# Input norm of a two-layer streaming encoder computed with tokens as rows; last-head results kept on the chip past a block; early features loaded in two places

## What is computed

```python
def rms_norm(x, g):
    xf = x.astype(jnp.float32)
    y = xf * lax.rsqrt(jnp.mean(xf * xf, axis=-1, keepdims=True) + EPS)
    return (y * g.astype(jnp.float32)).astype(x.dtype)

hp = rms_norm(yp, norm_g[l])                      # first step of layer 0
u, a_raw, b_raw, z_a, q_b, k_b, v_b, z_b = _split(h @ w_in, L0_SPLITS)
...
S_new, o_a = blocked_scan(gdn_block, S0, (q_a, k_a, v_a, g, beta), CHUNK)
...
y = jnp.concatenate([o_a, o_b], axis=-1) @ w_out  # layer 0
...
return o @ w_out, S_new                           # layer 1
```

## Time and profile before

| | |
|---|---|
| median of 3 runs | 3609.12 us (3608.56 to 3609.76) |
| profiled execution, its own time | 3610.31 us |
| its span, first to last instruction | 3608.6 us, 47321 instructions |
| mean granted TensorE clock | 0.99 of full |
| busy: TensorE, its weight loads | 3499.8, 2577.4 us |
| busy: VectorE, ScalarE, GpSimd | 1178.3, 1095.7, 533.1 us |

### The profile page before, as it was taken

How to read it: one execution, slowest core, us unless ns; L and a number is a source line. 1 busy time by engine, 2 the same in 40 slices (tenths; PEclk the granted TensorE clock), 3 DMA queues, 4 the chain that set the end, 5 groups by cost and what they waited for, 6 DMA issues and landing times. The chain is left out here.

```text
span 3608.6 us, 47321 instructions
## 1 busy us (share of the span) xinstructions
PE 3499.8 (97%) x16631; PEld 2577.4 (71%) x16631; DVE 1178.3 (33%) x2993; ACT 1095.7 (30%) x2794; POOL 533.1 (15%) x527
## 2 busy tenths in 40 slices
PE   8999999999799999999999998999999999899999
PEld 5777777777477878777766675677777777566676
DVE  3555545555223333333320234022222122220223
ACT  2443333333134334344210242122223222210242
POOL 3443345444000000000001002000000000011000
PEclk9999999999999999999999999999999999999999
DMA  5211411112412231122261102111111111371101
GB/s 145 60 38 32 31 28 34 32 37 84 102 39 43 44 42 30 43 46 90 89 198 47 36 13 79 41 30 44 39 50 44 37 36 33 117 230 47 35 1 48
DMA packets 246025, 206.85 MB, mean 57 GB/s; under 512 B 19903, under 2 KB 222943, under 8 KB 245831
## 3 DMA queue, kind: packets, MB, share of 16 engines
q1 hardware_dynamic: 239902, 194.16, 21.2%
q10 hardware_dynamic: 5936, 10.34, 0.8%
HBM read 158.49 MB, written 45.99 MB: 57 GB/s over the span
## 5 line engine op out<-in xcount | busy, mean ns | idle before, releaser
L497 PE MATMUL gdn_pj<-hT,Wb 128*128 128x352 f32 x1536 | 516.3, 462 | 3.0 <-PEq L45 3.0
L1999 PE MATMUL gla_pj<-hT,Wb 128*128 128x352 f32 x1536 | 471.9, 461 | 6.5 <-PEq L45 5.9
L1449 PE MATMUL band_pj<-hT,Wb 128*128 128x384 f32 (+1 forms) x1152 | 387.1, 465 | 16.8 <-PEq L45 13.8
L1999 PEld LDWEIGHTS gla_pj<-hT,Wb 128*128 128x128 f32 x1536 | 290.9, 191 | 156.8 <-issue 8.7
L497 PEld LDWEIGHTS gdn_pj<-hT,Wb 128*128 128x128 f32 x1536 | 266.3, 192 | 92.1 <-issue 5.5
L1449 PEld LDWEIGHTS band_pj<-hT,Wb 128*128 128x128 f32 x1152 | 207.2, 192 | 99.7 <-issue 19.5
L1995 PE MATMUL gla_pj<-gla_Wv,hT 128*128 128x256 f32 (+1 forms) x1152 | 266.8, 381 | 0.0
L1995 PEld LDWEIGHTS gla_pj<-gla_Wv,hT 128*128 128x128 f32 x1152 | 217.2, 190 | 31.8
L1634 ACT ACTIVATE band_E<-band_NS,band_nm 128x576 f32<-128x576 f32 (+9 forms) x136 | 89.8, 660 | 216.0 <-DVE band_nm L1712 215.9
L1211 POOL TENSOR_TENSOR x_kept<-gdn_AT,gdn_level 128x384 f32<-128x384 f32 x144 | 144.2, 1032 | 35.8 <-DVE gdn_TT L993 18.5
L1479 PE MATMUL band_pj<-Wb,hT 128*128 128x128 f32 x1152 | 144.2, 275 | 0.0
(11 more groups left out here) (410 smaller groups left out, 5490.3 us busy)
## 6 DMA issues: line engine op xcount, KB each, us to landing
Wb<-in_l_w_in_dram SPq DMA_DIRECT2D x96, 512.0 KB, 6.2
fin_xT<-x_features SPq DMA_DIRECT2D x16, 528.0 KB, 7.6
fin_R<-o_features SPq DMA_DIRECT2D x16, 528.0 KB, 9.7
Wb<-in_l_w_mkv_dram SPq DMA_DIRECT2D x8, 1024.0 KB, 5.5
Wb<-in_l_w_out_dram SPq DMA_DIRECT2D x16, 512.0 KB, 4.4
gla_Wv<-in_l_w_in_dram SPq DMA_DIRECT2D x8, 1024.0 KB, 5.4
o_features<-gla_OF ACTq DMA_DIRECT2D x14, 528.0 KB, 6.0
gdn_GB<-gate_rows SPq DMA_DIRECT2D x8, 544.0 KB, 3.7
```

What stands on the lines that cost most here:

```text
L497: mm = pe.matmul(pj[:, m % 2, 0:w], W[:, j, k, :], hT[:, k, c0:c0 + w], start=k == 0, stop=k == KD - 1)
L1449: mm = pe.matmul(out[:, 0:w], W[:, BAND_SLOT[j], k, :], hT[:, k, c0:c0 + w], start=k == 0, stop=k == KD - 1)
L1999: mm = pe.matmul(pj[:, m % 2, 0:w], W[:, SLOT[kind], k, :], hT[:, k, c0:c0 + w], start=k == 0, stop=k == KD - 1)
```

## The change

*Entry.* The norm is taken with tokens as rows, before the transposition. ScalarE squares the tile as it was loaded, with the row sum as second output, and takes logarithm and exponential of one column; VectorE scales the tile by it into `xN`; TensorE transposes both `xS` (for `x_kept`) and `xN` (for `hT`); VectorE multiplies the latter by the gain on its way out of PSUM. ScalarE copies seven of the nine tiles to `x_kept`, VectorE tiles 2 and 5. GpSimd and the matrix of ones are no longer used. 

```diff
+                def normed(t):
+                    pe.wait_ge(scaled, t + 1)
+                    wait(pe, h_out, t - 1)
                     for k in range(KD):
-                        mm = pe.matmul(PS[:, t % 2, 0:rows(t)], ones[:, :], sq[:, t % 2, k, 0:rows(t)], start=k == 0, stop=k == KD - 1)
-                    mm.then_inc(summed, 1)
+                        mm = pe.transpose(TH[:, t % 2, k, 0:r], xN[0:r, t % 2, 128 * k:128 * k + 128], ident[0:r, 0:r])
+                    mm.then_inc(h_turned, 1)
...
+                    act.wait_ge(x_ld[t], 16)
+                    wait(act, squared, t)
+                    act.activation(sq[0:r, :], xS[0:r, t, :], ACT.Square, accum_out=ss[0:r, t:t + 1]).then_inc(squared, 1)
+                    act.wait_ge(squared, t + 1)
+                    act.activation(rs[0:r, t:t + 1], ss[0:r, t:t + 1], ACT.Ln, scale=1.0 / D, bias=eps[0:r, 0:1]).then_inc(rooted, 1)
+                    act.wait_ge(rooted, t + 1)
+                    act.activation(rs[0:r, t:t + 1], rs[0:r, t:t + 1], ACT.Exp, scale=-0.5).then_inc(rs_ok, 1)
...
-                    pool.tensor_tensor(sq[:, t % 2, :, 0:rows(t)], xT[:, :, cols(t)], xT[:, :, cols(t)], ALU.mult).then_inc(squared, 1)
...
+                def out(t):
+                    dve.wait_ge(h_turned, t + 1)
+                    dve.tensor_tensor(hT[:, :, cols(t)], TH[:, t % 2, :, 0:r], g[:, :].unsqueeze(2).broadcast_to([128, KD, r]),
+                                      ALU.mult).then_inc(h_out, 1)
...
-                    for k in range(KD):
-                        mm = dve.scalar_tensor_tensor(hT[:, k, cols(t)], xT[:, k, cols(t)], g[:, k:k + 1], rs[:, t % 2, 0:r],
-                                                      ALU.mult, ALU.mult)
-                    mm.then_inc(h_out, 1)
+                    wait(dve, h_turned, t - 1)
+                    dve.tensor_scalar(xN[0:r, t % 2, :], xS[0:r, t, :], rs[0:r, t:t + 1], None, ALU.mult).then_inc(scaled, 1)
+                    if t:
+                        out(t - 1)
+                    if t in BY_DVE:
+                        dve.wait_ge(x_turned, t + 1)
+                        dve.tensor_copy(xT[:, :, cols(t)], TX[:, t % 2, :, 0:r]).then_inc(x_dve, 1)
```

```diff
-                sp.wait_ge(st_p, H_A * 16)
-                sp.wait_ge(st_s, H_A * 16)
-                sp.wait_ge(st_o, H_A * 32)
+                sp.wait_ge(st_p, (H_A - 1) * 16)
+                sp.wait_ge(st_s, (H_A - 1) * 16)
+                sp.wait_ge(st_o, (H_A - 1) * 32)
...
-                act.dma_start(state_p[last:H_A, :, :].rearrange("o d v -> d (o v)"), S[:, 0, :]).then_inc(st_p, 16)
-                act.dma_start(state_s[last:H_A, :, :].rearrange("o d v -> d (o v)"), Sn[:, :]).then_inc(st_s, 16)
...
-                act.dma_start(o_dram[128 * last:128 * H_A, 0:768], OF[:, 0:768]).then_inc(st_o, 16)
-                act.wait_ge(o_fin, last * 3 + 3)
-                act.dma_start(o_dram[128 * last:128 * H_A, 768:NTOK], OF[:, 768:NTOK]).then_inc(st_o, 16)
...
                 load_bias(0)
+                sp.dma_start(state_p[H_A - 1:H_A, :, :].rearrange("o d v -> d (o v)"), S3[:, 0, :]).then_inc(st_last, 16)
+                sp.dma_start(state_s[H_A - 1:H_A, :, :].rearrange("o d v -> d (o v)"), S3[:, 2, :]).then_inc(st_last, 16)
+                sp.dma_start(o_dram[128 * H_A - 128:128 * H_A, :], o_last[:, 0:NTOK]).then_inc(st_last, 16)
                 follow(0, 0, True)
...
+        def features(c, k):
+            c0, w = EARLY_PARTS[c]
+            return early[:, k, c0:c0 + w] if k < H_A - 1 else o_last[:, c0:c0 + w]
```

```diff
+        FIRST_K = 5
+        o_first = Wv[:, :, :].rearrange("p k n -> p (k n)")[:, 0:FIRST_K * 384].rearrange("p (k n) -> p k n", k=FIRST_K)
+        def features(c, k):
+            c0, w = EARLY_PARTS[c]
+            return hT[:, k, c0:c0 + w] if c or k >= FIRST_K else o_first[:, k, :]
...
                 for n, kind in enumerate(("z0", "z1", "q", "k")):
+                    if kind == "q":
+                        sp.wait_ge(proj_done, (H_C - 1) * NJ + LAST["v"] + 1)
+                        early_o(sp, o_dram, o_first, eo_ld[0][0], 0, 0, FIRST_K)
                     sp.wait_ge(proj_done, (H_C - 1) * NJ + LAST[kind] + 1)
+                    if kind == "k":
+                        early_o(sp, o_dram, hT, eo_ld[0][1], 0, FIRST_K, 8)
                     early_w(sp, W, early_ld, w_out, n, order[n])
-                early_o(sp, o_dram, hT, eo_ld, 0)
```

More of the change, by code:

```diff
@@ L129, in _ @@
                     pe.wait_ge(x_ld[t], 16)
-                    wait(pe, copied, t - 1)
+                    if t >= 2:
+                        if t - 2 in BY_DVE:
+                            pe.wait_ge(x_dve, by_dve[t - 1])
+                        else:
+                            pe.wait_ge(x_act, t - 1 - by_dve[t - 1])
                     for k in range(KD):
-                        mm = pe.transpose(TP[:, t % 2, k, 0:r], xS[0:r, t, 128 * k:128 * k + 128], ident[0:r, 0:r])
-                    mm.then_inc(turned, 1)
+                        mm = pe.transpose(TX[:, t % 2, k, 0:r], xS[0:r, t, 128 * k:128 * k + 128], ident[0:r, 0:r])
+                    mm.then_inc(x_turned, 1)
                     if t:
-                        total(t - 1)
-                total(TILES - 1)
+                        normed(t - 1)
+                normed(TILES - 1)
             @block.scalar
@@ L141, in _, with turned @@
                 act.preload_act_table_set("natural_log_exp_and_others")
-                def root(t):
-                    r = rows(t)
-                    act.wait_ge(summed, t + 1)
-                    wait(act, h_out, t - 1)
-                    act.activation(rs[:, t % 2, 0:r], PS[:, t % 2, 0:r], ACT.Ln, scale=1.0 / D, bias=eps[:, 0:1]).then_inc(rooted, 1)
-                    act.wait_ge(rooted, t + 1)
-                    act.activation(rs[:, t % 2, 0:r], rs[:, t % 2, 0:r], ACT.Exp, scale=-0.5).then_inc(rs_ok, 1)
+                def turned(t):
+                    if t in BY_DVE:
+                        return
+                    act.wait_ge(x_turned, t + 1)
+                    act.activation(xT[:, :, cols(t)], TX[:, t % 2, :, 0:rows(t)], ACT.Copy).then_inc(x_act, 1)
                 act.wait_ge(consts, 1)
@@ L153, in _ @@
                     r = rows(t)
[L154 to L155 removed]
+                    act.wait_ge(x_ld[t], 16)
[5 more added lines that the diff above has]
+                    act.activation(rs[0:r, t:t + 1], rs[0:r, t:t + 1], ACT.Exp, scale=-0.5).then_inc(rs_ok, 1)
                     if t:
[L157 to L158 removed]
+                        turned(t - 1)
+                turned(TILES - 1)
             @block.gpsimd
@@ L1292, in band @@
         OF = sb("OF", [128, NTOK])
-        early = sb("early", [128, 8, NTOK])
+        early = sb("early", [128, H_A - 1, NTOK])
         stage2 = sb("stage2", [128, 2, 384])
@@ L1419, in _ @@
                 for c in range(3):
-                    early_o(sp, o_dram, early, eo_ld, c)
+                    early_o(sp, o_dram, early, eo_ld[c], c, 0, H_A - 1)
                 for i in range(2):
@@ L1434, in _ @@
                 sp.wait_ge(st_v, PAIRS * 32)
+                sp.wait_ge(st_last, 48)
             @block.tensor
@@ L1487, in pair @@
                     steps = (stream(n + 1, 1 - p) if more else
-                             early_steps(pe, pj, (proj_out, PAIRS * J), early, eo_ld, W, EARLY_ORDER[0], early_ld, e_add, e_done))
+                             early_steps(pe, pj, (proj_out, PAIRS * J), features, [(eo_ld[c],) for c in range(3)], W, EARLY_ORDER[0], early_ld,
+                                         e_add, e_done))
                     per = FILL if more else FILL_LAST
@@ L2408, in early_store, with early_steps @@
         load_ahead(sp, [out_weights(W[:, order[n], :, :], late_ld[n], w_out, n, 8, 8)])
-def early_steps(pe, pj, free, o_early, o_ld, W, order, w_ld, added, done):
+def early_steps(pe, pj, free, features, o_ld, W, order, w_ld, added, done, first=8):
     for i, (n, c) in enumerate(EARLY):
@@ L2421, in early_steps @@
         if n == 0:
-            pe.wait_ge(o_ld[c], 16)
+            pe.wait_ge(o_ld[c][0], 16)
         for k in range(8):
-            mm = pe.matmul(pj[:, i % 2, 0:w], W[:, order[n], k, :], o_early[:, k, c0:c0 + w], start=k == 0, stop=k == 7)
+            if n == 0 and c == 0 and k == first:
+                pe.wait_ge(o_ld[c][1], 16)
+            mm = pe.matmul(pj[:, i % 2, 0:w], W[:, order[n], k, :], features(c, k), start=k == 0, stop=k == 7)
             if k == 7:
```

81 lines of the change are left out of this document (37 added, 44 removed).

## The result

The changed kernel takes **3575.26 us** (median of 4 runs, 3574.33 to 3580.13) against 3609.3 us before; the ratio is 0.9908, 95% interval 0.9893 to 0.9922. That is 34 us, where the forecast had 22.4, and it lies outside the forecast range of 3577 to 3594.

The account below looks back on a forecast made before the run. The prediction took TensorE, busy 97% of the span, as the bound. Entry -12.8, band start -12.0 and early features +2.4 made -22.4 us, from 3609.1 to 3586.7 us, with 3577 to 3594 expected eight times in ten.

Parts of the forecast that it names:

- the cold value: Entry: TensorE's transposes stay at the slow clock throughout, so the entry ends at 36.4 us, a gain of 12.8 us.
- The other prices: Entry, per piece: VectorE's multiply 1.22 us, its scaling 0.76 us, ScalarE's copy 1.02 us.
- warm entry: Rival, chance 0.22: the clock rises under transposes, VectorE bounds the entry, which gains 18.1 us; total 3581.4 us.
- the 0 I counted: Starts of the delta-rule and band blocks: cold TensorE work before and after, counted as no net change.
- the end I gave it: Start of the delta-rule block: the cold start's change in time was bounded by -1.2 and +1.7 us.
- Forecast 12.0: Start of the band block: without the wait for the last head's stores it starts 12.0 us earlier, between 11.7 and 12.4.
- The rival in which it doesn't shrink: Rival, chance 0.07: memory rows' stores land late, the band starts only 7 us earlier; total 3591.7 us.
- the three stores are covered in SyncE's queue: Band block: stores queued ahead of the next pair's weights are covered, since the third q projection comes 24 steps in.
- Ten steps directly behind the gate matmuls: Sign in layer 1: these steps, then 12 to 13 us idle that VectorE ends, then a granted clock of 0.5.
- The price was +2.4: Early features of layer 1: a loss of 2.4 us from 3.5 to 6.0 us cold; ends 0 and 4.7.
- The rival in which the feature wait was the bound: Rival, chance 0.05, layer 1: the 8.3 us wait comes back and nothing is lost; total 3576.0 us.
- Nothing later gives it back: Whole kernel behind the entry: the gains stay, since TensorE is the engine that the others wait for.

Follow-up runs that it names:

- e2_pe72: The changed kernel with 72 one-column transposes on TensorE ahead of the entry's first one; 3565.1 us.
- e8_start30: The changed kernel with 72 one-column TensorE transposes, thirty early matmuls instead of ten before the scores of layer 1's last head, and two VectorE adds moved up; 3552.7 us.
- e6_boundary: The kernel before with only the changed boundary: kept output and states, three stores in the band's SyncE program, seven blocks reloaded; 3593.9 us.
- e1: The changed kernel with 53 one-element memsets on VectorE in the entry, restoring its later program positions; 3586.7 us.
- e3: The kernel before with the changed entry alone; 3588.6 us.
- e4: The kernel before with 203 one-element memsets on VectorE in the entry; 3594.2 us.
- e5: The changed kernel with layer 1's first features loaded as before, one load of eight blocks behind the early weights; 3575.0 us.
- e10_pe36: The changed kernel with 36 one-column transposes on TensorE ahead of the entry; 3563.1 us.
- e12_both: The changed kernel with 36 one-column TensorE transposes ahead of the entry and thirty early matmuls before the first scores of layer 1's last head; 3548.0 us.
- e11_before_dve75: The kernel before with 75 one-element memsets on VectorE in the entry; 3595.9 us.

## Why the prediction was wrong

Faster was right, the size was not. The distance of 12.0 us between forecast and landmarks comes term by term: 8.4 in the entry, 1.4 in the cold start behind it, 1.0 for two effects that were in no term and nearly cancel (+12.1, -11.1; luck, since e2_pe72 has the first without the second and takes 3565.1 us), 0.4 at the band's start, 1.7 in the last head, and -0.9 in the rest.

*Entry: the step that failed is "So transposes seem not to raise it, and the changed entry has nothing else: I take the cold value."* The clock rose while TensorE did transposes alone, between 10.2 and 11.3 us, and so it did in every run with this entry, at 8.8 to 12.6 us. In the earlier trace rows small transposes and pauses stood between the restart (35.49) and the rise (44.9 by the clock records, 9.4 us later), and I took the transposes for the reason; which of the two it was, or neither, no run separates. That transposes hold the rate down no run shows either: in the changed kernel eight full loads take 0.85 to 0.91 us from 11.3 us to the entry's end, with nothing but transposes. The other prices held: VectorE's multiply took 1.22 us, its scaling 0.75, ScalarE's copy 1.01. The rival, warm entry, had the mechanism and was still 3.1 us short. It had the second multiply end at 15.5 us, with a clock that rises at 13, and it ended at 13.7; it left 14.7 us of VectorE's work behind it, and that took 13.3, since each instruction starts about 0.1 us before the one before it ends. In e8_start30, where the clock rose at 12.6, it was 13.3 too. VectorE bounds the entry, as that rival said: it has no pause between 12 and 27 us.

*Cold starts.* Both came out better than the 0 I counted: 1.4 us behind the entry, 0.2 past the end I gave it, and 0.8 of the 12.4 at the band's start (4.0 us of cold work there instead of 5.7). Behind the entry TensorE was at half rate for some 3 us instead of 6:

```profile
4.00:6.00 2.00, 1.12 (x6) 1.00 0.99 282
...
26.00:28.00 2.00, 0.41 (x7) 0.93 1.05 104
28.00:30.00 2.00, 2.00 (x4) 0.50 1.04 83
30.00:32.00 2.00, 2.00 (x7) 0.71 0.92 120
32.00:34.00 2.00, 2.00 (x8) 1.00 0.59 76
```

*Start of the band block: right.* Forecast 12.0, measured 11.6 to the first matmul. SyncE waited for no store of the last head, and VectorE's end set the start, 1.4 us behind it (forecast: 0.85 to 1.6). The rival in which it doesn't shrink is excluded. That the three stores are covered in SyncE's queue held as well (e6_boundary).

*Early features: right in kind; the price left out what absorbs it.* Ten steps directly behind the gate matmuls, 13.0 us idle, VectorE at its end, a cold clock behind: all as written. The price was +2.4, an estimate for 3.5 to 6.0 us of cold work; no run shows the 2.4. Behind the start of the scores the granted clock was 0.50 for 6.8 us in the changed kernel (3086.1 to 3092.9), for 5.5 in e1 (3097.9 to 3103.4) and for none in the kernel before. TensorE lost 3.1 us to the low clock, and the column shows 0.7, since TensorE's wait at the block's end, which was in no term, shrank by 2.4. Nor can the 3.1 be put to the edit: e3, e4 and e5 lose as much at a place that is as it was. The rival in which the feature wait was the bound is excluded by e5_no_early.

*What no term had.* "Nothing later gives it back" failed as a step: later stretches gave 12.1 more and took 11.1. I costed an instruction by what it does where it stands. It also moves everything behind it in its engine's program. The trace of before had the sign of the first: queue 14 with 26 packets inside a loop, and issue idle on VectorE of 12.9 us in all at one line that waits for nobody. That VectorE stands still until code of the next pass is fetched is my reading of the packets that start at each stall, at 2.4 us a pass (12.1 in five); how much of its program an engine holds, no run shows. Which positions are good I would not have been able to foretell, only that some 12 us stood on them in this loop, and that would have carried the range to the measured time. The stop in the band had no such sign in the trace of before.

## What to carry over

Before pricing an edit ahead of a loop, look for instruction-queue packets inside the loop and for idle time that is put down to "issue": what they cost depended here on the number of instructions ahead of it, so an edit far away could win or lose it (12.1 us with 53 memsets), and a few idle memsets or transposes test that in one run. Of a new wait that replaces an old one, ask what bounds its end: here a chain on other engines did, and the gain came only from moving real work in front of it, not from supplying its data sooner. A stretch in which an engine's clock stayed low doesn't show why; separate what it ran from the pauses between.

## What the hardware showed unexpectedly

- In the loop of the delta rule VectorE stands still for some 2.5 and 1.7 us at each pass or not at all, by the loop's position; 53 one-element memsets decide over 12.1 us.
- A 16 KB packet of TensorE's code that came behind bulk stores started some 12 us after the one before (1288.0 and 1300.0 us; 1288.3 and 1300.1 in e10_pe36); in that time the 16 DMA engines are busy and move 50 to 80 GB/s, a sixth to a quarter of the 328 GB/s they reach at 1300 us.
- With transposes of whole tiles alone TensorE came to its full rate (eight loads in 1.72 us at 8.5 us, in 0.91 at 11.3). While it was still at half rate (weight loads of 0.2 us, 4.9 to 10.2 us) the granted clock in the stretches reads 1.00 (the first of the rows on the cold start above), so early in the program durations tell the rate and that column doesn't: the trace has no clock record before 10.7 us.
- Behind pauses of much the same length (1490.4 to 1492.2 us in e10_pe36, 1490.2 to 1492.3 in e12_both) the clock stays up in one run and is low for 3.4 us in the other, which is the 1.7 us between their columns.
- A kernel can gain 0.4% from instructions that do nothing (e4_before_dve203, e11_before_dve75), which is twice what a measurement of this kernel can tell.
